# Banded attention with query tiles outermost and eight heads inside, normalised after the values

## The reference

```python
def _chunk_band_attention(q, k, v, bias):   # chunks of 64 tokens; a chunk sees itself and the 8 before it
    ...
    def one_chunk(n):
        sc = jnp.einsum("bhqd,bhkd->bhqk", qn, kb) * scale + bias      # scale = 64 ** -0.5
        sc = jnp.where((n + key_chunk_off) >= 0, sc, -1e30)
        p = jax.nn.softmax(sc, axis=-1)
        return jnp.einsum("bhqk,bhkd->bhqd", p, vb)
...
y = sigmoid(ga) * (oa @ w_a_out) + sigmoid(gb) * (ob @ w_b_out)        # ob is the banded attention's output
x = x + y @ w_o
```

## Time and profile before

| | |
|---|---|
| median of 3 runs | 2471.73 us (2471.42 to 2478.41) |
| profiled execution | 2477.05 us; its span 2475.3 us |
| busy: TensorE matmul, weight load | 2334.0 us (94%), 1879.6 us (76%) |
| busy: VectorE, ScalarE, GpSimd | 999.8 us (40%), 821.8 us (33%), 767.3 us (31%) |
| DMA | 201.67 MB, mean 81 GB/s |
| granted TensorE clock, mean | 0.968 of full |

### The profile page before, as it was taken

One profiled execution on the slowest core, in us unless ns is written; L12 is line 12 of the kernel. 1 busy time (PEld: TensorE's weight loads), 2 busy tenths in 40 slices (PEclk: granted clock), 3 DMA queues, 4 the chain that ended last, 5 costly groups with the idle time before them and its releaser, 6 DMA issues.

```text
span 2475.3 us, 29199 instructions
## 1 busy us (share of the span) xinstructions
PE 2334.0 (94%) x11860; PEld 1879.6 (76%) x11860; DVE 999.8 (40%) x1643; ACT 821.8 (33%) x1192; POOL 767.3 (31%) x210
## 2 busy tenths in 40 slices
PE   6999999989999979999999999999899899999998
PEld 3767778768888868787878788566588788788886
DVE  3355746541211257464646310624445345322202
ACT  3354533232222334142423323333323343322212
POOL 0223923323444422111111144021143432344342
PEclk9998999989999989999999999989899999999999
DMA  6412313413223221111111133112123332222221
GB/s 236 136 51 67 121 62 119 146 59 102 96 91 102 87 88 52 35 35 35 35 35 35 35 100 96 43 53 76 43 85 102 103 103 68 85 98 89 102 98 55
DMA packets 179906, 201.67 MB, mean 81 GB/s; under 512 B 3556, under 2 KB 170960, under 8 KB 179664
## 3 DMA queue, kind: packets, MB, share of 16 engines
q1 hardware_dynamic: 176848, 190.84, 23.8%
q10 hardware_dynamic: 2944, 9.22, 1.0%
HBM read 195.85 MB, written 4.19 MB: 81 GB/s over the span
## 4 chain that ended last, share of the span: by engine, by line
PE 81%; DVE 5%; ACT 3%; issue 2%; POOL 1%; DMA 1%; ACTq 0%; DVEq 0%; SPq 0%; POOLq 0%
PE ps L1913 19%; PE ps L1915 18%; PE ps L1914 18%; PE ps L2239 4%; PE ps L2013 3%; PE ps L2205 2%; PE ps L2436 1%; PE ps L2427 1%; POOL w_lo L651 1%; PE ps L2201 1%; PE ps L2434 1%; PE ps L1960 1%; ACT w_hi L724 1%; PE ps L1962 1%; PE ps L1961 1%
## 5 line engine op out<-in xcount | busy, mean ns | idle before, releaser
L651 POOL TENSOR_TENSOR w_lo<-raw,w_hi 128x2048 fp32r<-128x2048 f32 (+1 forms) x150 | 681.0, 4540 | 1506.7 <-ACT w_hi L724 1506.6
L1913 PE MATMUL ps<-h_hi,w_hi 128*128 128x512 f32 x1384 | 567.8, 410 | 22.7 <-POOL w_lo L651 8.5
L1915 PE MATMUL ps<-h_hi,w_lo 128*128 128x512 f32 x1384 | 547.2, 395 | 0.0
L1914 PE MATMUL ps<-h_lo,w_hi 128*128 128x512 f32 x1384 | 546.7, 395 | 0.0
L724 ACT ACTIVATE w_hi<-raw 128x2048 fp32r<-128x2048 f32 x150 | 285.6, 1904 | 404.9 <-PE ps L1915 396.3
L1913 PEld LDWEIGHTS ps<-h_hi,w_hi 128*128 128x128 f32 x1384 | 264.6, 191 | 105.4 <-issue 40.2
L1915 PEld LDWEIGHTS ps<-h_hi,w_lo 128*128 128x128 f32 x1384 | 264.4, 191 | 58.2
L1914 PEld LDWEIGHTS ps<-h_lo,w_hi 128*128 128x128 f32 x1384 | 265.3, 192 | 51.7 <-issue 1.2
L1913 PE MATMUL ps<-g_hi,w_hi 128*128 128x512 f32 x256 | 101.0, 394 | 0.0
L1448 DVE SCALAR_TENSOR_TENSOR score_b<-ps,bias_b 128x128 f32<-128x128 f32 (+1 forms) x64 | 31.4, 490 | 171.0 <-POOL bias_b L706 105.6
L1915 PE MATMUL ps<-g_hi,w_lo 128*128 128x512 f32 x256 | 100.4, 392 | 0.0
(11 more groups left out here) (379 smaller groups left out, 4071.7 us busy)
## 6 DMA issues: line engine op xcount, KB each, us to landing
raw<-w_in SPq DMA_DIRECT2D x48, 1024.0 KB, 5.2
raw<-w_down SPq DMA_DIRECT2D x27, 1024.0 KB, 4.9
raw<-ada_w SPq DMA_DIRECT2D x24, 1024.0 KB, 5.2
raw<-w_gate_up SPq DMA_DIRECT2D x22, 1024.0 KB, 5.1
raw<-w_up SPq DMA_DIRECT2D x16, 1024.0 KB, 5.2
raw<-w_mkv SPq DMA_DIRECT2D x8, 1024.0 KB, 5.4
raw<-w_out SPq DMA_DIRECT2D x4, 1024.0 KB, 5.2
raw<-w_a_out SPq DMA_DIRECT2D x4, 1024.0 KB, 4.9
```

Of the source, the lines that this page charges most:

```text
L651: nc.gpsimd.tensor_tensor(w_lo[:, split_at[u] % 2, 0:n], raw[:, u % 2, 0:n], w_hi[:, split_at[u] % 2, 0:n].bitcast(F32), ALU.subtract).the ...
L1913: T.matmul(out_, wh, hi, start=start, stop=False, skip_group_check=True)
L1914: T.matmul(out_, wh, lo, start=False, stop=False, skip_group_check=True)
L1915: return T.matmul(out_, wl, hi, start=False, stop=stop, skip_group_check=True)
```

## The change

- **Order.** In each group the query tile is now outermost and the eight heads inside: item n is tile n // 8, head n % 8. Items 0 to 7 have 128 keys, the last eight 512.
- **Look-ahead.** Scores run three items ahead instead of two, in banks 2 and 3; `score_b` and `prob_b` have three slots, the transposes two banks (4 and 5), the outputs two (6 and 7).
- **Sign.** VectorE writes the negated score and takes its minimum, which is then ScalarE's bias directly; the step at line 1452 goes.
- **Scaling.** Probabilities are not scaled. ScalarE leaves the row sums of eight heads side by side; when the eight outputs of a query tile lie in a bank, VectorE takes eight reciprocals at once and scales the whole bank into `tmp2` (`evict`).
- **Values token-major.** The stationary operand is `probT_b` (128 columns), the moving one 64 columns of `vb`. The scaled output is then turned back by four transposes for each query tile (`out_turned`), and split into `ob_hi` and `ob_lo` from there.
- **Fill.** Eight pieces (one unit) are left in a group, at items 0 to 7; the second unit is done as a whole behind the group. `next_hi` stands at item 10 only.
- **Biases.** All eight biases of a group are loaded in one transfer of 2 MB into `xT`. The residual goes to `x_kept` behind the norm `N_MIX` and comes back behind the last item of the second group. One memset masks the eight corners.
- **Banks.** The units of `band` and `bout` have fixed banks: 0, 2, 0, 2, 0, 6 and 0, 2, ... in turn, each with the one after it.
- Several semaphores are merged; the waits on them ask for the same events.

```diff
-    score_b = r("score_b", [P, 2, S])
-    bias_b = r("bias_b", [P, 2, S])
-    prob_b = r("prob_b", [P, 2, S])
+    score_b = r("score_b", [P, 3, S])
+    prob_b = r("prob_b", [P, 3, S])
...
+    for g in range(2):
+        fixed_bank.update({first[f"band{g}"] + i: b for i, b in enumerate([0, 2, 0, 2, 0, 6])})
+    fixed_bank.update({first["bout"] + i: 2 * (i % 2) for i in range(8)})
...  SyncE
+            sp.wait_ge(sem["n_t"], SCALED_BEFORE[N_MIX] + KT)
+            sp.dma_start(x_kept, xT[:, :, :].rearrange("p k c -> p (k c)")).then_inc(sem["x_out"], 16)
             for u in range(first["pair0"] + 2, first["aout"]):
                 load(u)
+            sp.wait_ge(sem["x_out"], 32)
+            load_bias(0)
             load_phase("aout")
+            load_phase("band0")
+            for u in range(first["band1"], first["band1"] + 4):
+                load(u)
+            sp.wait_ge(sem["b_neg"], 32)
+            load_bias(1)
+            for u in range(first["band1"] + 4, first["bout"] + 4):
+                load(u)
+            sp.wait_ge(sem["b_neg"], 64)
+            sp.dma_start(xT[:, :, :].rearrange("p k c -> p (k c)"), x_kept).then_inc(sem["x_back"], 16)
...  GpSimd
+                    if u == first[f"band{g}"] + 4:
+                        pool.wait_ge(sem["bias_in"], 16 * (g + 1))
+                        nc.gpsimd.memset(xT[0:CHUNK, :, S - CHUNK:S], -1e30).then_inc(sem["bias_ready"], 1)
...  ScalarE, band_attention
+                expo(0)
+                expo(1)
+                last_values()
+                for n in range(32):
+                    copy(n)
+                    if n + 2 < 32:
+                        expo(n + 2)
+                    if n >= 8 and n % 8 == 3:
+                        out_hi(n // 8 - 1)
+                    if n == 10:
+                        next_hi()
+                out_hi(3)
...  VectorE, band_attention
+                def neg(n):
+                    q, hh = n // 8, n % 8
+                    nk = (q + 1) * P
+                    dve.wait_ge(sem["b_scores"], N + n + 1)
+                    ...
+                    V.scalar_tensor_tensor(score_b[:, n % 3, 0:nk], ps[:, 2 + n % 2, 0:nk], -(DB ** -0.5), xT[:, hh, S - nk:S],
+                                           ALU.mult, ALU.subtract).then_inc(sem["b_neg"], 1)
+                    dve.wait_ge(sem["b_neg"], N + n + 1)
+                    V.tensor_reduce(b_min[:, n % 4:n % 4 + 1], score_b[:, n % 3, 0:nk], AX.X,
+                                    ALU.min).then_inc(sem["b_min_done"], 1)
+                def evict(q):
+                    dve.wait_ge(sem["b_values"], 8 * (i + 1))
+                    ...
+                    link(V.reciprocal(b_stat[:, q % 2, 1, :], b_stat[:, q % 2, 0, :]))
+                    V.tensor_tensor(tmp2[:, q % 2, :].rearrange("p (h c) -> p h c", c=DB),
+                                    ps[:, 6 + q % 2, :].rearrange("p (h c) -> p h c", c=DB),
+                                    over_width(b_stat[:, q % 2, 1, :], DB), ALU.mult).then_inc(sem["b_evicted"], 1)
...  TensorE, band_attention
+                def scores(n):
+                    if N + n >= 2:
+                        pe.wait_ge(sem["b_neg"], N + n - 1)
+                    T.matmul(ps[:, 2 + n % 2, 0:nk], qbT[row, hh // 2, tok(q)], kbT[row, hh // 2, 0:nk], ...)
+                def values(n):
+                    pe.wait_ge(sem["b_copied"], N + n + 1)
+                    ...
+                    for kt in range(q + 1):
+                        ins = T.matmul(ps[:, 6 + q % 2, hh * DB:(hh + 1) * DB], probT_b[:, n % 2, kt * P:(kt + 1) * P],
+                                       vb[:, kt, hh * DB:(hh + 1) * DB], start=kt == 0, stop=kt == q)
+                def out_turned(q):
+                    pe.wait_ge(sem["b_evicted"], 4 * g + q + 1)
+                    for i in range(4):
+                        ins = turn(ps[:, 6 + q % 2, i * P:(i + 1) * P], tmp2[:, q % 2, i * P:(i + 1) * P])
+                for n in range(3):
+                    scores(n)
+                last_values()
+                for n in range(32):
+                    if n + 3 < 32:
+                        scores(n + 3)
+                    if n < KT:
+                        piece(fill_unit, n)
+                    turned(n)
+                    if n:
+                        values(n - 1)
+                    if n >= 8 and n % 8 == 2:
+                        out_turned(n // 8 - 1)
+                values(31)
+                out_turned(3)
...
+            dve.wait_ge(sem["x_back"], 16 * KT + 16)
             out_phase("out2", N_XATTN)
```

More of the change, by code:

```diff
@@ L440, in build @@
         for j in range(x.tiles):
-            if first["f1"] <= u < first["ada_b"]:
-                banks.append(j)
+            if u in fixed_bank:
+                banks.append(fixed_bank[u] + j)
             else:
@@ L1174, in _ @@
                 next_hi()
-                attention(f"band{g}", prob_b, probT_b, 1.0, ob_hi, (14, 29), lambda: (store_values(u + 5, 1), next_hi()))
+                band_attention(g, lambda: (store_values(u + 5, 1), next_hi()))
             for n, (kind, j) in enumerate(GATED):
@@ L1466, in out_lo @@
                     if kind == "mem":
-                        tiles = [(2 * (g - 12) + j, out_bank(n, j), 12 + 2 * (g - 12) + j) for j in range(2)]
+                        tiles = [(2 * (g - 4) + j, out_bank(n, j), 4 + 2 * (g - 4) + j) for j in range(2)]
                     else:
-                        tiles = [(g - (4 if kind != "one" else 0), out_bank(n), g)]
+                        tiles = [(g, out_bank(n), g)]
                     for k, bank, count in tiles:
@@ L1807, in _ @@
             for g in range(2):
-                attention(f"band{g}", prob_b, 1.0, ob_hi, ob_lo)
+                band_attention(g)
             def y2_lower(k):
@@ L2202, in scores @@
                         ins = T.matmul(ps[:, bank + 1, 0:C], qT[:, h, tok], kT[:, h, S:S + C], start=True, stop=True)
-                    elif what == "band":
-                        row, tile = slice((h % 2) * DB, (h % 2 + 1) * DB), (h % 8) // 2
-                        ins = T.matmul(ps[:, bank, 0:nk], qbT[row, tile, tok], kbT[row, tile, 0:nk], start=True, stop=True)
                     else:
@@ L2212, in turned @@
                 def turned(n):
-                    prob = {"one": prob1, "band": prob_b, "mem": prob_m}[items[n][0]]
+                    prob = {"one": prob1, "mem": prob_m}[items[n][0]]
                     pe.wait_ge(sem["at_prob"], n + 1)
@@ L2232, in values @@
                     else:
-                        before = g if what == "band" else g - 1
-                        if before > 0:
-                            pe.wait_ge(sem["at_out_lo"], before)
-                        v, pT = (v1, probT1) if what == "one" else (vb, probT_b)
+                        if g > 1:
+                            pe.wait_ge(sem["at_out_lo"], g - 1)
+                        v, pT = v1, probT1
                         nk = keys_of(n) // P
@@ L2487, in _ @@
                     pe.wait_ge(sem["o_done"], 2 * p + 2)
-            def projected(name, hi, lo, done, base):
-                for j in range(4):
-                    wide_gemm(gated(name, "proj", j), hi, lo, ready=after(done, base) if j == 0 else None)
             wide_gemm(gated("aout", "sig", 3), h_hi, h_lo)
-            projected("aout", oa_hi, oa_lo, sem["oa_lo_done"], 0)
+            for j in range(4):
+                wide_gemm(gated("aout", "proj", j), oa_hi, oa_lo, ready=after(sem["oa_lo_done"], 0) if j == 0 else None)
@@ L2498, in _ @@
             for g in range(2):
                 u = first[f"band{g}"]
-                for j in range(2 * g, 4):
+                for j in range(g, 4):
                     wide_gemm(u + j, h_hi, h_lo)
@@ L2531, in _ @@
                 piece(u + 1, k)
[L2532 removed]
+            pe.wait_ge(sem["table_in"], 48)
             pe.wait_ge(sem["rb_done"], 1)
```

173 lines of the change are left out of this document (107 added, 66 removed).

## The result

The changed kernel takes **2437.62 us** (median of 4 runs, 2436.95 to 2440.66), the kernel before 2471.81 (4 runs): a ratio of 0.9858, 95% interval 0.984 to 0.9876. The profiled executions took 2440.66 and 2477.05 us.

What follows compares the result with a forecast made beforehand. TensorE bounds the kernel; two groups with their units go from 194.0 to 172.0 us, and added waits leave net -19.2 on the profiled 2477.05: 2457.9, set at 2454 us against the median. Own range 2445 to 2463, with rivals 2438 to 2471.

Steps and rivals of the forecast that it cites:

- the price of the blocks: TensorE in the groups, start to start: transposes 0.26 to 0.57 us, values 0.37 to 1.02, scores 0.41 to 1.05, piece 1.59.
- Values token-major ... 160 records: Values matmuls in a group: 0.112 us a record taken, 22.8 us in all; 8.6 less at the lower end.
- The wait ahead of the last `out_turned`: At a group's end, TensorE waits 1.3 us for the eviction and three handoffs, with nothing in between.
- Start of `band0`: TensorE waits 1.0 us for an eviction, because the last unit before ends in banks 3 and 0.
- Third scores: The third scores block in front costs 0.41 us plus about 0.5 waiting for VectorE: 0.9 a group, outside the stretch.
- Clock full throughout: In the groups, no half-clock tails, since the waits that emptied TensorE at the ends are gone but for 1.3 us.
- the check's price at full clock: Block prices summed for a group of the kernel before: 83.8 us, against 94.0 and 95.4 in the trace.
- A: Rival: the clock falls to half in items without pieces, 8 to 31; +78 - 19, 2536 us; 8%.
- B: Rival: only the group-end tails stay slow, some 7 us of half clock at each end; +7, 2461 us; 22%.
- C: Rival: four-engine handoffs lose 0.4 us in each of 48 items without piece; -19 + 19, 2472 us; 12%.
- D: Rival: the values' matmuls stream at 64 columns, records 0.05 us apart; -17 more, 2436 us; 5%.
- Transfers hidden: Residual and bias loads, 6.3 us for each 2 MB, finish before they are needed and cost nothing.

Runs made afterwards that it cites:

- the first probe: The changed kernel with 216 float32 matmuls added ahead of the bands, weight shapes alone and alternating, nothing else on TensorE; 2527.96 us, one run.

## Why the prediction was wrong, and where it was right

*The failed step is the price of the blocks.* "I price TensorE in blocks, from one block's start to the next's, since this holds the change of work too" is sound for the kernel before; it was wrong to carry the prices over to a loop whose neighbours have other shapes. The prices of the earlier trace rows hold the switches, which belong to pairs of neighbours. Before, an item went through 64x128, 128x64 and 128x128, three switches, four with a piece. Token-major values have 128x128 weights like the transposes and the pieces, and two switches are left. "Values token-major ... 160 records, 22.2 + 160 x 0.004" counted the record (right: 0.112) and left the switch in. Undone by itself it is worth 6.3 us a group, one switch of 0.197 an item, and 12.6 us of the time, out of the 16.4 by which the forecast was too high.

*The rest of the miss in the groups*, 75.3 forecast against 72.3 with the values channel-major: the piece 1.50 in place of 1.59, because the block behind it now has weights of its shape (0.7); the rounding at item 10 hidden (0.5); values 0.7; eviction 1.0 in place of 1.3; the last copy free (0.2); turning back and transposes 0.4. Every one was set on the dear side. Together they are 2.8 of the 3.0 a group.

Point by point:
- Scores, 29 blocks at 22.2: measured 22.21. Right.
- Eight pieces as a whole unit at 10.7: 10.9. Right.
- The wait ahead of the last `out_turned`, 1.3: 1.02. The waits for `qbT` and `sig_b` gone: right, no idle at 1609.46.
- Start of `band0`, 1.0: 1.07 (1472.94 to 1474.24 is 1.30, in place of 0.23 for such a step before). Third scores, 0.9 a group: 0.4 (1474.24 to the first group is 69.20 us, before 68.79).
- Clock full throughout: right in the outcome, but for another reason than the text gives. It took the scaling and the late rounding for the causes of the half-clock tails. Done one at a time in the kernel before, neither part gains anything, and the rounding put back in the changed one costs 3.4. Putting back the order of values and transposes costs 52, or 16.6 with the rounding at a better place.
- So what holds the other 21.6 of the 34.2 us is in part open. An account by the two traces, in whose two groups with their units 40.2 us went: 12.6 the shape (measured by the run), 14.6 fewer waits (16.6 to 2.0), and by difference, as estimates, some 10 of work at half clock (the 194.0 less the waits and less 2 x 83.8, the check's price at full clock) and 3 of other work. Among the waits are 4.8 us for the one output bank, which was not put back by itself. The forecast had waits and half clock right as a whole (10 to 12 us a group, and 2.8 and 1.8 behind).
- Rivals. A (clock falls in the thin items) did not come, but with one reordering it did, behind one wait of 0.53 us and for 78.5 us, so this kernel is not far from it. The reading of the earlier trace rows, that the transposes ran at half clock until the clock rose, holds: in the first probe a transpose at 0.50 takes the same 421 ns. B (tails stay slow) and C (round trip binds) did not come; for C there is not one wait for `probT_b` or `prob_b` in TensorE's waits of the group. D gave nearly the right time (2436), but that is luck: the records are 0.111 apart, not 0.054.
- Transfers hidden: right. TensorE has no wait behind them. The biases took 10.3 us in the median where 6.3 was assumed, within the slack given:

```profile
xT<-bias_band SPq DMA_DIRECT2D x2, 2048.0 KB, 10.3
```

The range was too narrow below because shrinking blocks stood in it as a remark, without a price, though the rows had one: in the earlier trace rows a transposes block of one record of 0.107 costs 0.26, and the other 0.15 was not asked about.

## What to carry to other kernels

Price a block with its neighbours' shapes: a change of the weights' rows or columns cost 0.14 to 0.2 us on TensorE each time here, so give neighbouring matmuls one shape, and put those that need 64 rows in pairs on the two halves, where the second is free. Look at the record durations inside a block before trusting its total; the difference is either a wait or a switch. In a stretch of short blocks place everything that can hold a copy where the blocks are long, since half a microsecond of wait stood, in one group of two, ahead of half a clock for the rest of the stretch. And a part that gains nothing alone can gain in company: where waits and half clock follow on each other, taking one away leaves the next.

## What the runs showed of the hardware that was not expected

- Two float32 matmuls on the two row halves run at once (48 records in 2.68 us, 0.056 each), on the two column halves too (2.77 us); the records of a pair start 0.007 us apart.
- The first matmul behind a change of shape starts 0.20 to 0.21 us behind the last record ahead of it in place of 0.11, and its own first record takes another 0.21, or 0.16 with 64-column weights or 64 moving columns.
- The clock can fall with TensorE never idle: in the first probe it went to 0.50 at 1527.3, with no gap since 1466.56, some 2 us after short matmuls that change shape every time had followed 25 us of 512-column ones, which change shape too. Short ones in turn at 128 columns had held 1.00 for 19 us before (1477.96 to 1497.12). In the kernel with the values first it stayed at 0.50 for 78.5 us, in the first 61 of which TensorE was busy throughout.
